# Stick-breaking attention: the sum of key blocks 1 to 3 is made once for the last two query blocks, and ScalarE takes two casts behind moved work

## What is computed

```python
z = jnp.einsum("bhtd,bhsd->bhts", qb, kb).astype(jnp.float32) * scale
mask = s_idx < t_idx
log_keep = jnp.where(mask, jax.nn.log_sigmoid(-z), 0.0)
tail = lax.cumsum(log_keep, axis=3, reverse=True)
between = jnp.concatenate([tail[..., 1:], jnp.zeros_like(tail[..., :1])], axis=-1)
a = jnp.where(mask, jnp.exp(jax.nn.log_sigmoid(z) + between), 0.0)
outs.append(jnp.einsum("bhts,bhsd->bhtd", a.astype(vb.dtype), vb))
```

## Time and profile before

| | us |
|---|---|
| three runs, median | 1520.82 |
| lowest, highest | 1519.12, 1520.83 |
| the profiled execution | 1519.06 |
| its span | 1517.2 |
| PE busy in the span | 1492.2 (98%) |
| PE's granted clock, mean | 0.997 |

### The profile page before, as it was taken

One profiled execution on the slowest core, in us unless ns is written; L12 is line 12 of the kernel. 1 busy time (PEld: TensorE's weight loads), 2 busy tenths in 40 slices (PEclk: granted clock), 3 DMA queues, 4 the chain that ended last, 5 costly groups with the idle time before them and its releaser, 6 DMA issues.

```text
span 1517.2 us, 19993 instructions
## 1 busy us (share of the span) xinstructions
PE 1492.2 (98%) x6806; PEld 1234.5 (81%) x6806; DVE 849.6 (56%) x1297; ACT 677.0 (45%) x1020; POOL 798.1 (53%) x986
## 2 busy tenths in 40 slices
PE   9999999999999999999989999999999999999996
PEld 6888888888888888887878888888788888888885
DVE  7999996555555411258974665646755555511145
ACT  6777886433333322247463542635633333322243
POOL 5343344666666755466255154452566666655452
PEclk9999999999999999999999999999999999999998
DMA  4111111332222422234132222321222222332221
GB/s 176 57 61 59 47 56 62 105 98 96 97 97 97 142 96 95 69 108 157 56 140 96 86 103 98 132 86 40 97 97 97 97 97 97 118 111 97 90 84 56
DMA packets 41798, 142.14 MB, mean 94 GB/s; under 512 B 4240, under 2 KB 8464, under 8 KB 41744
## 3 DMA queue, kind: packets, MB, share of 16 engines
q1 hardware_dynamic: 40592, 138.69, 26.8%
q10 hardware_dynamic: 1152, 2.74, 0.5%
HBM read 139.32 MB, written 2.10 MB: 93 GB/s over the span
## 4 chain that ended last, share of the span: by engine, by line
PE 93%; DVE 3%; ACT 2%; POOL 1%; issue 1%; DMA 0%; DVEq 0%; SPq 0%; ACTq 0%
PE bank L558 26%; PE bank L561 26%; PE bank L562 26%; PE bank L836 3%; PE bank L841 3%; PE bank L840 3%; PE bank L636 2%; POOL wl L521 1%; PE bank L616 1%; PE bank L647 1%; PE bank L646 1%; PE bank L617 1%; DVE xl L1064 1%; ACT wh L1625 0%; DVE sumsq L1058 0%
## 5 line engine op out<-in xcount | busy, mean ns | idle before, releaser
L505 POOL TENSOR_TENSOR wl<-raw,wh 128x256 fp32r<-128x256 f32 x752 | 615.7, 851 | 476.7 <-ACT wh L1625 476.7
L558 PE MATMUL bank<-xh,wh 128*128 128x512 f32 (+1 forms) x1160 | 451.6, 389 | 5.1 <-POOL wl L521 4.1
L562 PE MATMUL bank<-xh,wl 128*128 128x512 f32 (+1 forms) x1160 | 450.2, 388 | 0.0
L561 PE MATMUL bank<-xl,wh 128*128 128x512 f32 (+1 forms) x1160 | 450.0, 388 | 0.0
L1625 ACT ACTIVATE wh<-raw 128x1024 fp32r<-128x1024 f32 (+1 forms) x212 | 235.0, 1108 | 476.8 <-PE bank L558 394.3
L558 PEld LDWEIGHTS bank<-xh,wh 128*128 128x128 f32 x1160 | 217.9, 188 | 51.9 <-POOL wl L521 5.0
L562 PEld LDWEIGHTS bank<-xh,wl 128*128 128x128 f32 x1160 | 217.8, 188 | 44.8
L561 PEld LDWEIGHTS bank<-xl,wh 128*128 128x128 f32 x1160 | 217.9, 188 | 43.7
L521 POOL TENSOR_TENSOR wl<-raw,wh 128x256 fp32r<-128x256 f32 x160 | 128.7, 837 | 192.6 <-ACT wh L1625 192.6
L1084 DVE TENSOR_TENSOR x<-x,bank 128x512 f32<-128x512 f32 x56 | 38.5, 687 | 254.4 <-PE bank L562 254.4
L558 PE MATMUL bank<-yh,wh 128*128 128x512 f32 x352 | 136.9, 389 | 0.0
(11 more groups left out here) (220 smaller groups left out, 2334.2 us busy)
## 6 DMA issues: line engine op xcount, KB each, us to landing
raw<-in_w SPq DMA_DIRECT2D x180, 512.0 KB, 3.2
raw<-in_w SPq DMA_DIRECT2D x32, 704.0 KB, 4.0
rc<-in_w SPq DMA_DIRECT2D x16, 512.0 KB, 4.2
w_end<-in_w SPq DMA_DIRECT2D x8, 512.0 KB, 4.4
rb<-in_w SPq DMA_DIRECT2D x8, 512.0 KB, 6.3
x<-in_xT SPq DMA_DIRECT2D x4, 512.0 KB, 6.6
pin<-in_pT ACTq DMA_DIRECT2D x2, 512.0 KB, 3.2
outT<-x SPq DMA_DIRECT2D x4, 256.0 KB, 3.4
```

Of the source, the lines that this page charges most:

```text
L505: last = nc.gpsimd.tensor_tensor(wl[:, slot, cols], part[:, cols], wh[:, slot, cols].bitcast(F32), ALU.subtract)
L558: first = mm(out, ah_, bh_, start=start, stop=False, skip_group_check=True)
L561: mm(out, ah_, bl_, start=False, stop=False, skip_group_check=True)
L562: return mm(out, al_, bh_, start=False, stop=stop, skip_group_check=True)
```

## The change

The blocks 1, 2 and 3 are summed once for query blocks 2 and 3, where the last stage needs them all. DVE's `last_three` adds `sp[1]`'s last 256 columns and the pair (block 2 for query block 2, `both` for query block 3) into a new tile `three_f`; one operation can read that pair since `both` now lies in spare columns of `sp[2]`, as its parts did in `sph[2]`. ACT casts it to `three_h`, DVE subtracts to `three_l`. The last stage of `cumulate` is now two matmuls of 512 columns (block 0), two of 128 (block 1, query block 1) and two of 256 (`three_h`, `three_l`), and waits for `three_low` too.

The cast of block 0, 512 columns, goes from DVE to ACT. ACT's order is changed around its two new casts: with half 0 the weight tile is cast ahead of them; with half 1 q's move comes ahead of them and both weight tiles and k's cast behind. The other edits give `sp[2]` its slices.

```diff
-            sp = [sb(f"sp{j}", [T - j * P], F32, ph) for j in range(TB)]
+            sp = [sb(f"sp{j}", [T if j == TB - 2 else T - j * P], F32, ph) for j in range(TB)]
...
-            both = sb("both", [P], F32, ph)
+            both = sp[TB - 2][:, 2 * P:3 * P]
...
+            three_f = sb("three_f", [2 * P], F32, ph)
+            three_h, three_l = sb("three_h", [2 * P], F32R, ph), sb("three_l", [2 * P], F32R, ph)
...
@@ cumulate
                     if j == TB - 3:
                         pe.wait_ge(both_low, s + 1)
+                    if j == 0:
+                        pe.wait_ge(three_low, s + 1)
+                        for out, parts in (
+                                (Z[0][:], (sph[0], spl[0])),
+                                (Z[0][:, P:2 * P], (sph[1][:, 0:P], spl[1][:, 0:P])),
+                                (Z[0][:, 2 * P:T], (three_h, three_l))):
+                            for part in parts:
+                                last = mm(out, (negtri if parts[0] is sph[0] else negones)[:], part[:], start=False,
+                                          stop=True, skip_group_check=True)
+                        last.then_inc(cum_done, 1)
+                        continue
...
@@ slot, on DVE
+                def last_three():
+                    two = sp[TB - 2][:].rearrange("p (a t) -> p a t", t=2 * P)[:, :, 0:P]
+                    dve.wait_ge(sp_full, 4 * s + 3)
+                    vec.tensor_tensor(three_f[:].rearrange("p (a t) -> p a t", t=P),
+                                      sp[1][:, P:3 * P].rearrange("p (a t) -> p a t", t=P), two, ALU.add)\
+                        .then_inc(three_full, 1)
+
+                def last_three_low():
+                    dve.wait_ge(three_high, s + 1)
+                    low(three_l[:], three_f[:], three_h[:], three_low)
...
                     if jj == 2:
                         last_two()
-                softplus_high(TB - 1)
+                        last_three()
+                last_three_low()
                 softplus_low(TB - 1)
...
@@ slot, on ACT
-                for tile in tiles:
-                    tile_high(*tile)
-                if more and half == 1:
+                if half == 0:
+                    for tile in tiles:
+                        tile_high(*tile)
+                elif more:
                     move_q(p + 1, 1 - par_)
-                    split_qk(p + 1, 1, 1 - par_)
+                act.wait_ge(three_full, s + 1)
+                copy(three_h[:], three_f[:], three_high)
+                act.wait_ge(sp_full, 4 * s + 4)
+                copy(sph[0][:], sp[0][:], sp_high)
+                if half == 1:
+                    for tile in tiles:
+                        tile_high(*tile)
+                    if more:
+                        split_qk(p + 1, 1, 1 - par_)
                 act.wait_ge(both_full, s + 1)
```

More of the change, by code:

```diff
@@ L244, in program @@
         both_full, both_high, both_low = (sem(n) for n in ("both_full", "both_high", "both_low"))
+        three_full, three_high, three_low = (sem(n) for n in ("three_full", "three_high", "three_low"))
         cum_done, a_full, a_high, a_low = sem("cum_done"), sem("a_full"), sem("a_high"), sem("a_low")
@@ L1187, in softplus @@
                     dve.wait_ge(z_ln, 4 * s + jj + 1)
-                    vec.scalar_tensor_tensor(sp[j][:], sp[j][:], SOFTPLUS_LINEAR, Z[j][:, 0:T - j * P], ALU.min, ALU.max)\
+                    part = sp[j][:, 0:T - j * P]
+                    vec.scalar_tensor_tensor(part, part, SOFTPLUS_LINEAR, Z[j][:, 0:T - j * P], ALU.min, ALU.max)\
                         .then_inc(sp_full, 1)
@@ L1193, in softplus_high @@
                     dve.wait_ge(sp_full, 4 * s + jj + 1)
-                    vec.tensor_copy(sph[j][:, 0:T - j * P], sp[j][:]).then_inc(sp_high, 1)
+                    vec.tensor_copy(sph[j][:, 0:T - j * P], sp[j][:, 0:T - j * P]).then_inc(sp_high, 1)
                 def softplus_low(jj):
@@ L1199, in softplus_low @@
                     cols = slice(0, T - j * P)
-                    low(spl[j][:, cols], sp[j][:], sph[j][:, cols], sp_low)
+                    low(spl[j][:, cols], sp[j][:, cols], sph[j][:, cols], sp_low)
                 def last_two():
-                    vec.tensor_tensor(both[:], sp[TB - 2][:, P:2 * P], sp[TB - 1][:], ALU.add).then_inc(both_full, 1)
+                    vec.tensor_tensor(both, sp[TB - 2][:, P:2 * P], sp[TB - 1][:], ALU.add).then_inc(both_full, 1)
                     dve.wait_ge(both_full, s + 1)
-                    vec.tensor_copy(both_h, both[:]).then_inc(both_high, 1)
+                    vec.tensor_copy(both_h, both).then_inc(both_high, 1)
                     dve.wait_ge(both_high, s + 1)
-                    low(both_l, both[:], both_h, both_low)
+                    low(both_l, both, both_h, both_low)
+                def last_three():
[7 more added lines that the diff above has]
+                    low(three_l[:], three_f[:], three_h[:], three_low)
                 def weights_low(jj):
@@ L1212, in weights_low @@
                     dve.wait_ge(a_high, 4 * s + jj + 1)
-                    low(al[j][:], sp[j][:], ah[j][:], a_low)
+                    low(al[j][:], sp[j][:, 0:T - j * P], ah[j][:], a_low)
                 softplus(0)
@@ L1715, in exponential @@
                     act.wait_ge(z_done, 4 * s + jj + 1)
-                    nc.scalar.activation(sp[j][:], Z[j][:, 0:T - j * P], ACT.Exp).then_inc(z_exp, 1)
+                    nc.scalar.activation(sp[j][:, 0:T - j * P], Z[j][:, 0:T - j * P], ACT.Exp).then_inc(z_exp, 1)
                 def ln_one_plus(jj):
@@ L1720, in ln_one_plus @@
                     act.wait_ge(z_exp, 4 * s + jj + 1)
-                    nc.scalar.activation(sp[j][:], sp[j][:], ACT.Ln, bias=1.0).then_inc(z_ln, 1)
+                    part = sp[j][:, 0:T - j * P]
+                    nc.scalar.activation(part, part, ACT.Ln, bias=1.0).then_inc(z_ln, 1)
                 for t in range(TB + 1):
@@ L1743, in slot @@
                         act.wait_ge(cum_done, 4 * s + jj + 1)
-                        nc.scalar.activation(sp[j][:], Z[j][:, 0:T - j * P], ACT.Exp).then_inc(a_full, 1)
+                        nc.scalar.activation(sp[j][:, 0:T - j * P], Z[j][:, 0:T - j * P], ACT.Exp).then_inc(a_full, 1)
                     if jj:
                         act.wait_ge(a_full, 4 * s + jj)
-                        copy(ah[j + 1][:], sp[j + 1][:], a_high)
+                        copy(ah[j + 1][:], sp[j + 1][:, 0:T - (j + 1) * P], a_high)
                 if more and half == 0:
```

## The result

| | before | after |
|---|---|---|
| median of 13 runs | 1520.51 | 1523.66 |
| lowest, highest | 1519.12, 1520.83 | 1522.14, 1525.36 |

The ratio is 1.0022, 95% interval 1.0014 to 1.0029: 3.15 us slower (2.1 to 4.4 by the interval), just above the 3.0 us that the prediction called a difference. It had forecast +1.8 us, 1522.6 with a range of 1518.6 to 1525.2.

A forecast was written before the change was run, and what follows sets the result against it. TensorE was taken to bound the kernel: -2.72 saved, waits of 0.77 + 2.34 (odd slots), 1.07 (slot 14) and 0.36 (slots 0 and 15) sum to +1.8 us on 1520.82, so 1522.6; range 1518.6 to 1525.2.

The forecast's parts named there:

- What bounds the kernel, and where the change would be paid: TensorE busy 98% of the span; savings pay in full, stalls cost in full, mainly at `values` in odd slots.
- the walk: Operation-by-operation schedule of odd slot 5, carried on to slot 14: `al` ends 114.37, PE stalls 0.39 us at `values`.
- The durations without a row: VectorE's new 256-column operations: 0.42 us assumed, the middle of 128 columns (0.29) and 384 (0.55).
- PE's saving: Last stage of the cumulation: a 128-column pair (0.17) replaces a 384-column pair (0.35); 0.17 less per slot, -2.72 us.
- The step: Costing of the last stage's narrowed pair from profile rows: 108.08 - 107.91 = 0.17 us for a pair of 128.
- The waits of the odd slots: PE stalls for `al` before `values`: 0.77 us in slot 1, 0.39 each in slots 3 to 13 (2.34).
- Slot 14: PE waits 1.07 us for `spl0` before the last stage; between 0.2 and 1.6.
- Even slots 2 to 12: More projection work on PE, so `spl0` is ready 0.2 to 0.3 us in time; no cost, a thin margin.
- Slots 0 and 15: VectorE already last or nearly, before the last stage: +0.25 and +0.11 us, together 0.36, between -0.5 and +1.
- B: Rival: no stall at `values`, as DVE and POOL interleave better; -2.2 us, 1518.6; chance 0.19.
- C: Rival: even slots' margin goes, six wait 0.30 each, slot 14 0.57 more; +2.4 us, 1525.0; chance 0.14.
- D: Rival: in the last stage a 128-column pair takes 0.24, saving only 0.11 a slot; 1523.6; chance 0.04.

## Why the prediction was nearly right

- **What bounds the kernel, and where the change would be paid**: right. PE's seven waits for `al` came where the walk had them, with the length that it gave: 0.40 in slot 5 for 0.39. POOL starts 2.44 us later for 2.4; `spl0` in slot 5 ends at 106.56 + 0.69 = 107.25, 2.28 us before PE's last stage, for "over 2".
- **The durations without a row**: `three_f` and `three_l` were taken at 0.42 and measured 0.418 and 0.420 in the median.
- **PE's saving was mis-sized**: -2.72 forecast, -2.01 in the kernel that has nothing else. The step took the pair of 128 from 107.91 to 108.08 and ended there. The 0.05 stands in the next row of that same stage: the matmul of 384 that starts at 108.08 takes 0.23 to its successor, where a 384 otherwise takes 0.17 to 0.18. That is 0.7 of the 1.2 us by which the forecast was short. The formula of the Trainium skill, "TensorE: Matmul & The Clock Gate", section "Back-to-back issue gap" (213 ns a slot), was further off than the rows; the measured saving is 0.12. The same section warns that the formula under-counts for narrow matmuls and gives some 81 ns for one of 128 columns; the runs show 0.11 us.
- **The waits of the odd slots**: 0.77 + 2.34 forecast. Measured from the cumulation to `values`: slot 1 lost 0.60, slot 5 and most others 0.40, and each wait another 0.05 in the matmul behind it, which I hadn't counted. Together about 3.4, so 0.3 more.
- **Slot 14**: 1.07 forecast, 0.97 measured. That the walk, eleven operations long, was out by only a tenth is partly luck: it let `three_f` pass ahead of POOL at its free 0.42 and had a turn lost before `spl0`. POOL came first, 0.4 us earlier than walked, so `three_f` took 0.99 and `spl0` was free.
- **Even slots 2 to 12**: no wait, as forecast, with 0.44 to 0.50 to spare where I gave 0.2 to 0.3 and called it thin.
- **Slots 0 and 15**: +0.25 and +0.11 forecast for their waits; 0.21 and 0.09 came. In slots 14 and 15 the last stage, behind its wait, takes 1.03 instead of 0.92, which had no term: 0.2 in all. A further 0.2 is spread over the stretches of projections, a few hundredths each, and stays unexplained.
- **Rivals**: B (no wait) and C (waits in even slots) are refuted by the trace, D (the narrow pair saves less) was right in its kind: it gave 0.11 a slot for the real 0.12, and I had held it at 0.04 against the rows at 107.91. With D's saving the time was 1523.6, and 1523.66 was measured; that it fits so well is luck, since D makes the saving 0.25 us too small in all, where the waits were 0.3 us short.

So the mechanism and the places were right, and the size was short mainly by the price of what stands behind a narrow matmul and behind a wait.

## What to carry to other kernels

When a cast is moved ahead of others on an in-order engine, follow what the delayed one triggers: here a tile that nobody needed soon set when POOL worked, and POOL's turns moved from a stretch of DVE with slack to the one that PE waits for. The same operations, with one cast at another place, made 4.3 us of difference. And cost a narrowed matmul up to the start of the second one behind it, not of the first.

## What the runs showed of the hardware

- A fp32r matmul of 128 columns, among others that each have their weight load, costs 0.11 to 0.12 us, as does one of 256 (0.12). Where it stands behind a wider one, half of that shows in its own row (0.06), the other half in the next.
- After a wait a matmul of 512 columns costs 0.34 to the next one instead of 0.29 in `values`, and the last stage takes 1.03 instead of 0.92 in slots 14 and 15 of the changed kernel. A short wait of PE costs 0.05 to 0.1 us more than its length.
- DVE operations with two SBUF sources and POOL's take turns, by whole operations; DVE's casts do too (384 columns: 0.90 us in slot 14 for 0.35), while softplus, with a PSUM source, took its free 0.68 there. Halving POOL's operations to 128 columns shortened a pair of `k_pack` subtractions from 2.42 to 1.72 us.
- After the same wait of 2.5 us the granted clock averaged 0.83 or 0.84 over 10 us in nine profiled executions and stayed at 1.00 in two; it makes 1.6 us in a single execution's time, half of the change's effect.
